# All eight score products of the cross attention ahead of its softmax, maxima kept in four columns

## What is computed

```
def cross_attention(hn, memn, w_q, w_kv, q_gain, k_gain, w_o):
    bsz, seq, _ = hn.shape
    q = rms_norm((hn @ w_q).reshape(bsz, seq, X_HEADS, HEAD_DIM), q_gain)
    k, v = jnp.split(memn @ w_kv, 2, axis=-1)
    k = rms_norm(k.reshape(bsz, -1, X_HEADS, HEAD_DIM), k_gain)
    v = v.reshape(bsz, -1, X_HEADS, HEAD_DIM)
    s = jnp.einsum('bshd,bmhd->bhsm', q, k).astype(jnp.float32) * HEAD_DIM ** -0.5
    p = jax.nn.softmax(s, axis=-1).astype(v.dtype)
    o = jnp.einsum('bhsm,bmhd->bshd', p, v).reshape(bsz, seq, X_WIDTH)
    return o @ w_o
```

## Time and profile before

| | us |
|---|---|
| median of 3 runs | 1390.5 (1389.57 to 1391.21) |
| profiled execution, its own time | 1391.4 |
| its span | 1389.6 |
| PE busy | 1315.8 (95% of the span) |
| DVE busy | 640.7 (46%) |
| ACT busy | 420.3 (30%) |
| POOL busy | 89.7 (6%) |

### The profile page before, as it was taken

The page is one execution under the profiler, slowest core; times in us unless marked ns, Lnnn a source line. Parts: engine busy times, 40 slices in busy tenths (PEclk is TensorE's granted clock), DMA queues, the critical chain, the costliest instruction groups (busy, mean ns, idle before and its releaser), DMA issues.

```text
span 1389.6 us, 48246 instructions
## 1 busy us (share of the span) xinstructions
PE 1315.8 (95%) x21406; PEld 1078.9 (78%) x21406; DVE 640.7 (46%) x1405; ACT 420.3 (30%) x831; POOL 89.7 (6%) x139
## 2 busy tenths in 40 slices
PE   6997898999999999879889999999999999999997
PEld 4754545777777686554569999999999999999996
DVE  6875512102421237642235555555555555455554
ACT  4424412100102122451223334333333333333332
POOL 0350000000000017000100000000000000000000
PEclk9996899999999999779989999999999999999999
DMA  8530033243341064100658999999999999999980
GB/s 357 198 122 1 1 151 121 105 182 149 124 182 61 18 253 152 62 1 3 269 234 346 427 426 426 425 428 426 425 427 427 426 426 427 426 426 426 427 355 32
DMA packets 32577, 357.68 MB, mean 257 GB/s; under 512 B 3683, under 2 KB 5347, under 8 KB 6412
## 3 DMA queue, kind: packets, MB, share of 16 engines
q1 hardware_dynamic: 30368, 353.78, 61.5%
q10 hardware_dynamic: 2156, 3.18, 0.6%
HBM read 355.88 MB, written 1.06 MB: 257 GB/s over the span
## 4 chain that ended last, share of the span: by engine, by line
PE 89%; DVE 5%; ACT 2%; issue 2%; POOL 1%; DMA 0%; DVEq 0%; ACTq 0%; POOLq 0%
PE bank L2083 28%; PE bank L1544 27%; PE bank L2099 14%; PE bank L2030 5%; PE bank L2145 2%; PE bank L1552 2%; PE bank L1816 2%; PE bank L2070 1%; PE bank L1880 1%; PE bank L1693 1%; PE bank L1564 1%; DVE ring L960 1%; PE bank L1637 1%; PE bank L1855 1%; ACT ring L573 1%
## 5 line engine op out<-in xcount | busy, mean ns | idle before, releaser
L2083 PE MATMUL bank<-R,ring 128*64 128x80 f32 x11264 | 421.8, 233 | 1.2 <-DVEq L942 0.7
L2083 PEld LDWEIGHTS bank<-R,ring 128*64 128x64 f32 x11264 | 403.1, 137 | 8.8 <-issue 8.8
L1544 PE MATMUL bank<-ring 128*128 128x256 f32 (+1 forms) x1408 | 368.9, 421 | 8.6 <-DVE ring L960 4.9
L1544 PEld LDWEIGHTS bank<-ring 128*128 128x128 f32 x1408 | 269.3, 193 | 107.1 <-issue 67.5
L833 ACT ACTIVATE ring<-ring 128x1024 f32<-128x1024 f32 x176 | 186.0, 1057 | 146.6 <-PE bank L2099 146.6
L2099 PE MATMUL bank<-zz,ring 128*64 128x80 f32 x5632 | 224.9, 233 | 0.0
L2099 PEld LDWEIGHTS bank<-zz,ring 128*64 128x64 f32 x5632 | 208.0, 137 | 0.0
L1506 DVE SCALAR_TENSOR_TENSOR zz<-zz,bank 128x80 f32<-128x80 f32 x176 | 41.9, 238 | 198.7 <-PE bank L2083 198.2
L1485 DVE COPY ring<-ring 128x1024 f32<-128x1024 f32 x177 | 121.6, 687 | 1.9 <-DVE R L1475 1.9
L1489 DVE COPY ring<-ring 128x1024 f32<-128x1024 f32 x177 | 121.5, 686 | 0.1
L829 ACT ACTIVATE X<-bank 128x80 f32<-128x80 f32 x176 | 41.8, 238 | 245.9 <-PE bank L2083 245.9
(11 more groups left out here) (297 smaller groups left out, 1032.3 us busy)
## 6 DMA issues: line engine op xcount, KB each, us to landing
ring<-moe_w_dram SPq DMA_DIRECT2D x177, 1536.0 KB, 10.2
ring<-ffn_w_dram SPq DMA_DIRECT2D x11, 3072.0 KB, 10.0
ring<-w_in_dram SPq DMA_DIRECT2D x6, 2048.0 KB, 10.5
ring<-w_out_dram SPq DMA_DIRECT2D x4, 2048.0 KB, 8.5
ring<-w_x_dram SPq DMA_DIRECT2D x2, 3072.0 KB, 10.7
ring<-w_small_dram SPq DMA_DIRECT2D x2, 2896.0 KB, 9.6
ring<-w_in_dram SPq DMA_DIRECT2D x2, 2144.0 KB, 20.6
ring<-bias_rows_dram ACTq DMA_DIRECT2D x1, 1536.0 KB, 8.0
```

The lines of the kernel that those rows point to most:

```text
L1544: i = pe.matmul(out_ap, a, b, start=(k == 0), stop=(k == n - 1))
L2083: e = pe.matmul(pb[out_bank][c0:c0 + 64, 0:CAP], half[:, P * k + c0:P * k + c0 + 64], xg[:, k], start=(k == 0), stop=(k == KT - 1), tile_p ...
```

## The change

The units get a bank each (`XS_BANKS`), the two calls of `xscores` stand together ahead of the loop, DVE keeps unit k's maximum in columns k of `nmx` (which has four pairs of columns) and waits for the units of the sparse attention only, and ACT reads the maximum from there.

```
+XS_BANKS = [6, 7, 4, 3]
...
         for u in range(4):
-            a(f"xs{u}_", 6 + u % 2, 0)
+            a(f"xs{u}_", XS_BANKS[u], 0)
             a(f"xpT{u}_", u % 2)
...
-            def probs(buf, b, src, scale, to):
+            def probs(buf, b, src, scale, to, m):
 
                 return act.activation(s_of[buf][:, b * src.shape[-1]:(b + 1) * src.shape[-1]], src, ACT.Exp,
-                                      bias=nmx[:, buf, b:b + 1], scale=scale, accum_out=to)
+                                      bias=nmx[:, m, b:b + 1], scale=scale, accum_out=to)
...
                     banks.wait(dve, f"xs{k}_{l}")
-                    dve.wait_ge(sem["probs_ready"], u - 1)
-                    own(dve.tensor_reduce(nmx[:, u % 2], ps(f"xs{k}_{l}")[:].rearrange("p (b s) -> p b s", b=2), AX, ALU.max, negate=True))
-                    dve.tensor_scalar(nmx[:, u % 2], nmx[:, u % 2], SCALE, None, ALU.mult).then_inc(sem["max_ready"], 1)
+                    dve.wait_ge(sem["probs_ready"], 20 * l + 16)
+                    own(dve.tensor_reduce(nmx[:, k], ps(f"xs{k}_{l}")[:].rearrange("p (b s) -> p b s", b=2), AX, ALU.max, negate=True))
+                    dve.tensor_scalar(nmx[:, k], nmx[:, k], SCALE, None, ALU.mult).then_inc(sem["max_ready"], 1)
...
                 xscores(0)
+                xscores(1)
                 for k in range(4):
...
                     done(nm, e)
-                    if k == 1:
-                        xscores(1)
                     if k:
                         xvalues(k - 1)
```

More of the change, by code:

```diff
@@ L737, in _ @@
                         for b in range(2):
-                            e = probs(at(v), b, s_of[at(v)][:, b * nk:b * nk + nk], 1.0, sums[:, i, b, hh:hh + 1])
+                            e = probs(at(v), b, s_of[at(v)][:, b * nk:b * nk + nk], 1.0, sums[:, i, b, hh:hh + 1], at(v))
                         e.then_inc(sem["probs_ready"], 1)
@@ L796, in _ @@
                             e = probs(k % 2, b, ps(f"xs{k}_{l}")[:, 256 * b:256 * b + 256], SCALE,
-                                      sums[:, i, 0, 2 * b + hp:2 * b + hp + 1])
+                                      sums[:, i, 0, 2 * b + hp:2 * b + hp + 1], k)
                         e.then_inc(sem["probs_ready"], 1)
```

## The result

| | before | changed |
|---|---|---|
| median, first comparison (6 runs each) | 1390.19 us (1389.57 to 1391.21) | 1380.74 us (1380.14 to 1382.12) |
| ratio | | 0.9935, 95% interval 0.9925 to 0.9946 |
| profiled execution, its own time | 1391.4 us | 1380.6 us |
| its span | 1389.6 us | 1378.8 us |

A forecast was written before the change was run, and what follows sets the result against it. TensorE (PE) was taken as the bound, 89% of the chain. Two cross attentions at 3.78 us save 7.6 us: 1391.4 becomes 1383.8, the median 1390.5 becomes 1382.9; middle 1383.4 us, range 1381.8 to 1386.8.

The forecast's parts named there:

- The stall: Cross attention, each layer: late score products delay the exponentials of unit 2; moved ahead, these start 3.78 us earlier.
- the sum: Two cross attentions at 3.78 us each, 7.6 us, taken off the profiled 1391.4 us or the median 1390.5.
- Costs at nothing: Cross attention: moved score products (1.13 us) fit PE's 2.0 us of idle time; banks and maxima edits cost nothing.
- The clock in the block: Cross attention: PE's clock stays at 2.4 GHz, so 3.78 us a layer; at 1.2 GHz the gain is 2.44.
- Rival 1: Cross attention: clock still falls (gain 2.44 us a layer), or most earlier runs lacked the fall (2.38); 1385.7 us, chance 0.18.
- The shift arrives: Behind both blocks, dense layer and expert loop keep PE busy and pass the gain on; expert weight loads cost nothing.
- Rivals 2 to 4: Fall moves into output products (1386.4, 0.07); clock stays down in dense work (1404, 0.04); late products held back (1390.5, 0.03).
- the term of 1.1 us: Range's allowance below 1382.9 us for a clock falling more kindly in the stages behind, giving 1381.8.

The follow-up runs named there:

- the filled kernel: The kernel before plus four unread score products a layer in the cross attention's 2.0 us of PE idle time; 1386.0 us against 1389.1, ratio 0.9974.

## Why the prediction was right or wrong

**The stall.** Right. The late scores were the wait that ended last, and exponentials 2 now start 0.48 us behind copy 0, the price that the prediction gave a copy. A block gained 3.77 us where the sum has 3.78.

**Costs at nothing.** Right: the moved products run in PE's idle time, which fell from 2.00 to 1.14 us. All eight take 2.00 us where the prediction had about 2.3: it had added the 1.13 us of four twice, and in one stretch the second four add only 0.87. The maxima are 0.8 us apart, and the edit of the maxima changed nothing by itself (ratio 1.0002) nor when it was taken out (blocks 10.97 and 10.96 us).

**The clock in the block.** Right. Rival 1's bound of 1.40 us for the clock is what the filled kernel measured (1.39), but that case did not occur: three more executions of kernels with the late order show the fall as the first did, and none with the new order does. The rule of the Trainium skill, "TensorE: Matmul & The Clock Gate", section "A second HAM failure mode: psum-queue depth-cycling", as the prediction read it, would have kept the fall here. The trace contradicts that reading for this block: four groups of transposes and values still change banks with gaps between them, at a clock of 1.00. The page tells of another kernel, in bf16.

**The shift arrives.** Right for both layers. 0.2 us of it is missing between the blocks: 449.47 to 449.49 us in three executions with the old order in layer 0, 449.65 to 449.71 in five with the new one. In the traces the products stand at the same place behind layer 0's output products, within 0.02 us, up to the scores of layer 1's sparse attention 337.1 us behind them. There the clock falls, by its records 0.3 us later than with the old order, and the 0.2 us arises behind that point; how was not separated.

**Rivals 2 to 4.** None occurred: the output products take 7.13 us in both layers, at full clock.

**What failed: the absolute time and the range.** The step is "Range: down from 1382.9 by 1.1 us for a clock that falls more kindly in the stages behind". The three medians of the changed kernel are 1380.7, 1381.1 and 1382.7; two lie below 1381.8. The sum started from one execution at 1391.4 us, and I allowed 1.1 us for everything outside the block. The next profiled execution of the same kernel had a span of 3.8 us less, of it 2.4 ahead of the first scores and 1.1 in the routing stage, with less time at 1.2 GHz in both. So the term of 1.1 us was too small by more than half. The spread of three runs, 1.6 us, had been taken for the spread of the kernel; over more runs it is 1387.1 to 1391.5, and the time goes with the granted clock: the three runs at a mean of 0.965 took 1390.8 to 1391.5 us, the nine at 0.970 1387.1 to 1388.6. I also looked for the clock's luck only behind the block, while two thirds of those 3.8 us stood ahead of it.

The measured median lies 2.7 us under the forecast. Of this 0.8 us is the base: the middle of two numbers, 1391.0, where the runs of before in that comparison had a median of 1390.2. The other 1.9 us is gain beyond the two blocks (9.4 against 7.6). The later comparisons gave 8.0 and 7.7 us, and the interval of the first ratio (0.9925 to 0.9946) only just reaches the 7.5 us of the blocks. That its excess is the clock's luck in those six runs is the likely reading and is not shown run by run.

The lowest run of the kernel before in the later comparisons is 1387.1; a range that allowed for that would have reached down to 1387.1 − 7.6 = 1379.5, below every measured median.

## What to carry to other kernels

When a group of products feeds a softmax on other engines, issue the next group ahead of the wait, not behind it, if banks are free; then see whether buffers that look like part of the fix are needed at all. A gain of 0.5% is better read from the pieces of a timeline, which repeated to 0.01 us here, than from two medians, which differed by 2 us for one and the same kernel. PE's idle gaps can cost twice: their own length, and the products at half clock behind them. Products without a use in such a gap can pay, but not in every gap: of the four tried here those of 2.0 and 1.6 us paid, that of 2.1 us did by the pieces of the timeline, and that of 3.5 us gained nothing that showed.

## What the runs showed of the hardware beyond the expectation

- PE's clock can be kept up by useless products in gaps that were idle anyway: four in a gap of 2.0 us removed a fall in each cross attention (2.08 us back to 1.13), three, six and four in each sparse attention took the kernel from 0.9949 to 0.9882 of the time before in one comparison. The six, in a gap of 3.5 us, left the fall behind them at 10.2 us.
- Dense PE work does not always bring the clock back: from 112 to 130 us PE is busy 16.7 of 18 us at a mean granted clock of 0.57, in the changed kernel's windows above.
- The clock's first rise came between 21.3 and 24.8 us in the twelve profiled executions, and the 32 products around it took 8.5 to 10.2 us: a difference of up to 1.7 us between executions. The two compared above are 1.3 us apart there and still 1.35 us apart 80 us later.
